# Moving the head-norm sums of an HGRN2 layer between two input-projection halves, in eight narrow matmuls instead of six wide ones

## The chip, the cores and the metric

The kernel runs on one core of a Trainium2 chip. The metric is the device time of one execution in microseconds; the kernel before was timed three times, with a median of 1609.88 us (1609.36 to 1610.61). Engines are called PE (matrix), DVE (vector), ACT (scalar), POOL and SP (the queue that starts most transfers).

## The reference, cut to what matters

One step of a two-layer encoder trunk for 256 + 64 = 320 frames, width 1024, in float32. Layer 0 is a mix of two recurrences and a dense feed-forward part; layer 1 is an HGRN2 recurrence and a top-2-of-8 expert feed-forward part. The change touches only the end of the HGRN2 mixer:

```
proj = h @ w_in_c                      # 1024 -> 4096: q, f, i, g, 8 heads of 128 each
o, s = chunk_gated_linear_attention(silu(q), k(f), i, log_f(f), s0)
o = o * rsqrt(mean(o*o over a head's 128) + 1e-5) * hgrn_norm_w      # rms_norm
out = (o * silu(g)) @ w_out_c          # 1024 -> 1024
```

## The kernel before, in words

Features lie on the 128 partitions, frames in the free dimension, so a head is one block of 128 x 320, and half of the heads (0 to 3 or 4 to 7) one block of 128 x 1280. Every dense matrix comes from memory in tiles of 1024 x 256. A tile is worked on in two halves (512 rows each): ACT rounds a half to a shorter float (`half_rounded`, line 1945), DVE subtracts it from the original (`half_rest`, line 1167), and PE takes three products, high by high, low input by high weight, high input by low weight (lines 518 to 520). A half is 24 matmuls of 320 columns. The input of a product is split in the same way: for the output projection ACT copies each head to its high part (`output_rounded`, line 2263) and DVE subtracts (`output_rest`, line 1658).

The input projection `in_c` has 16 tiles, 0 to 15, the output projection `out_c` four, which the code also counts on as 16 to 19. Tile 15 of `in_c` gives the last two heads of the gate g. The recurrence's steps are written between the halves of the tiles 8 to 15, the same order by hand on each engine. At its end DVE adds the parts of the output (`outputs_of(h)`, line 1642), ACT squares them (`squares(h)`, line 2248), PE sums the squares over the partitions by a matmul with a matrix of ones (`hgrn_sums(h)`, line 968), ACT takes Ln and then Exp with scale -0.5 (`root_mean(h)`, lines 2254 and 2258), DVE multiplies (`normed`, line 1648) and applies the gate (`gated`, line 1651). h is the half of the heads.

PE writes to eight banks of PSUM (a bank holds 512 columns of float32), and `take` hands them out in turn. It waits for a count on a semaphore that says that the bank's previous user has been read: the owner and the count are given when the bank is taken. `turn[0] += 2` skips two banks. The first two tiles of `out_c` take their four banks together, before the first of their matmuls. Semaphores are shared between stages; in the tables of order below `attention_b` counts the added outputs, `attention_osq` the squares, `attention_rms` what ACT has read or made of the sums, `in_c_done` the projected banks that ACT has emptied, `dense_lo` the weight halves ready, `in_lo` the heads split.

## Time and profile before

| | |
|---|---|
| median of three runs | 1609.88 us (1609.36 to 1610.61) |
| the profiled execution, its own time | 1610.61 us |
| its span from first to last instruction | 1608.8 us |
| PE busy | 1484.3 us (92% of the span) |
| DVE busy | 1161.5 us (72%) |
| ACT busy | 944.9 us (59%) |
| granted PE clock, mean over the span | 0.966 of full |
| HGRN2 end with `out_c` (716 to 762 us): PE busy | 42.97 of 46 us |

Times are from the start of the span. In rows of a timeline the columns are the start, the time from the first start to the last end of the merged instructions, the engine and line, the operation with output and inputs, the count, and in brackets how long the engine was idle before it and who released it. PE records of float32 matmuls with ones appear twice for each matmul of the program. "x12" at line 968 is six matmuls.

### The profile page before, as it was taken

The numbers are of one execution on the slowest core, as the hardware profiler recorded it, in microseconds if no ns is written. First come the engines' busy times: TensorE is split into PE (matmuls) and PEld (weight loads), VectorE is DVE, ScalarE is ACT, GpSimd is POOL, SyncE is SP. The second block draws the span as 40 slices with busy tenths as digits, with TensorE's granted clock in tenths as the row PEclk, the third lists the DMA queues.
The fourth block names the chain that finished last, engine by engine and source line by source line (L and its number), as shares of the span: only waits on it lengthen the run. The fifth ranks groups of instructions, "written<-read, shape, count | busy, mean of one in ns | idle before, by whom it ended". The sixth has DMA issues, their size and how long they took to land.

```text
span 1608.8 us, 28958 instructions
## 1 busy us (share of the span) xinstructions
PE 1484.3 (92%) x11188; PEld 1325.4 (82%) x11189; DVE 1161.5 (72%) x1562; ACT 944.9 (59%) x1238; POOL 75.2 (5%) x147
## 2 busy tenths in 40 slices
PE   7889967899999899999599999999999999999992
PEld 7879967799999798988477888887888888788881
DVE  5574846455543458965488898898889989898994
ACT  5453114433332468544467777877788777877872
POOL 8200000000000000000000000000000000000000
PEclk9999988999999999999689999999999999999996
DMA  8411002244444343322389999999999999999982
GB/s 245 149 53 57 4 2 76 87 142 156 157 138 151 106 131 119 106 80 89 132 328 352 398 367 390 381 357 396 332 398 366 382 387 344 396 335 404 367 299 80
DMA packets 162030, 371.70 MB, mean 231 GB/s; under 512 B 10152, under 2 KB 85840, under 8 KB 161936
## 3 DMA queue, kind: packets, MB, share of 16 engines
q1 hardware_dynamic: 159120, 360.14, 61.4%
q0 software_dynamic: 2448, 8.91, 2.1%
q8 instruction: 69, 1.13, 0.3%
q10 hardware_dynamic: 368, 1.31, 0.2%
q14 instruction: 25, 0.20, 0.0%
HBM read 360.10 MB, written 10.24 MB: 230 GB/s over the span
## 4 chain that ended last, share of the span: by engine, by line
PE 76%; DVE 12%; issue 6%; ACT 4%; DMA 1%; DVEq 0%; SPq 0%; POOLq 0%; POOL 0%; ACTq 0%
PE bank L1093 9%; PE bank L1094 9%; PE bank L1095 9%; PE bank L518 9%; PE bank L520 9%; PE bank L519 9%; DVE w_lo L1809 4%; PE bank L602 4%; PE bank L1117 3%; PE bank L1119 3%; PE bank L1118 3%; DVE wd_lo L1167 1%; PE bank L839 1%; PE bank L834 1%; PE bank L890 1%
## 5 line engine op out<-in xcount | busy, mean ns | idle before, releaser
L1809 DVE TENSOR_TENSOR w_lo<-moe_ring,w_hi 128x1024 fp32r<-128x1024 f32 (+1 forms) x560 | 608.0, 1156 | 42.4 <-ACT w_hi L2363 42.3
L2363 ACT ACTIVATE w_hi<-moe_ring 128x1024 fp32r<-128x1024 f32 (+1 forms) x560 | 532.6, 1014 | 84.3 <-PE bank L1119 51.6
L1167 DVE TENSOR_TENSOR wd_lo<-arena,wd_hi 128x1024 fp32r<-128x1024 f32 x142 | 171.0, 1208 | 189.2 <-ACT wd_hi L1945 188.8
L518 PE MATMUL bank<-in_hi,wd_hi 128*128 128x320 f32 x880 | 279.3, 317 | 23.6 <-DVE in_lo L1180 17.0
L1093 PE MATMUL bank<-w_hi,xe_hi 128*128 128x512 f32 (+1 forms) x768 | 288.6, 376 | 1.4 <-DVE xe_lo L1843 1.4
L1094 PE MATMUL bank<-w_hi,xe_lo 128*128 128x512 f32 (+1 forms) x768 | 286.6, 373 | 0.0
L1095 PE MATMUL bank<-w_lo,xe_hi 128*128 128x512 f32 (+1 forms) x768 | 286.1, 372 | 0.0
L519 PE MATMUL bank<-in_lo,wd_hi 128*128 128x320 f32 x880 | 275.6, 313 | 0.0
L520 PE MATMUL bank<-in_hi,wd_lo 128*128 128x320 f32 x880 | 275.4, 313 | 0.0
L1945 ACT ACTIVATE wd_hi<-arena 128x1024 fp32r<-128x1024 f32 x142 | 148.3, 1047 | 194.4 <-PE bank L520 185.9
L518 PEld LDWEIGHTS bank<-in_hi,wd_hi 128*128 128x128 f32 x880 | 168.8, 192 | 28.6 <-issue 21.7
L519 PEld LDWEIGHTS bank<-in_lo,wd_hi 128*128 128x128 f32 x880 | 169.0, 192 | 0.1
L520 PEld LDWEIGHTS bank<-in_hi,wd_lo 128*128 128x128 f32 x880 | 168.6, 192 | 0.0
L1093 PEld LDWEIGHTS bank<-w_hi,xe_hi 128*128 128x128 f32 x768 | 145.0, 189 | 27.5 <-DVE xe_lo L1843 1.8
L1095 PEld LDWEIGHTS bank<-w_lo,xe_hi 128*128 128x128 f32 x768 | 144.6, 188 | 26.1
L1094 PEld LDWEIGHTS bank<-w_hi,xe_lo 128*128 128x128 f32 x768 | 144.9, 189 | 25.1
L1117 PE MATMUL bank<-w_hi,gt_hi 128*128 128x512 f32 x256 | 101.2, 395 | 2.3 <-DVE w_lo L1809 2.3
L1119 PE MATMUL bank<-w_lo,gt_hi 128*128 128x512 f32 x256 | 99.8, 390 | 0.0
L1118 PE MATMUL bank<-w_hi,gt_lo 128*128 128x512 f32 x256 | 99.7, 389 | 0.0
L602 PE MATMUL bank<-arena 64*64 64x64 f32 (+1 forms) x2128 | 72.4, 230 | 16.3 <-DVE arena L1457 9.9
L602 PEld LDWEIGHTS bank<-arena 64*64 64x64 f32 x2128 | 70.3, 145 | 18.0 <-DVE arena L1457 10.3
L518 PE MATMUL bank<-hid_hi,wd_hi 128*128 128x320 f32 x240 | 74.2, 309 | 2.5 <-DVE hid_lo L1658 1.5
(354 smaller groups left out, 1721.4 us busy)
## 6 DMA issues: line engine op xcount, KB each, us to landing
moe_ring<-in_moe_w SPq DMA_DIRECT2D x216, 1024.0 KB, 8.4
moe_ring<-in_moe_w SPq DMA_DIRECT2D x64, 768.0 KB, 4.7
arena<-in_ffn_w SPq DMA_DIRECT2D x30, 1024.0 KB, 5.4
arena<-in_w_in_c SPq DMA_DIRECT2D x16, 1024.0 KB, 5.3
arena<-in_w_in_ab SPq DMA_DIRECT2D x13, 1024.0 KB, 5.9
arena<-in_w_out_ab SPq DMA_DIRECT2D x4, 1024.0 KB, 5.8
arena<-in_w_out_c SPq DMA_DIRECT2D x4, 1024.0 KB, 4.9
arena<-in_ffn_w SPq DMA_DIRECT2D x4, 768.0 KB, 4.2
```

Source lines behind the costliest of these rows:

```text
L518: pe.matmul(b[:, 0:T], w_[0][:, cols], x_hi, start=start, stop=False)
L519: pe.matmul(b[:, 0:T], w_[0][:, cols], x_lo, start=False, stop=False)
L520: return pe.matmul(b[:, 0:T], w_[1][:, cols], x_hi, start=False, stop=stop)
L602: mm = pe.matmul(b[rows, col:col + right.shape[-1]], left[rows], right[rows], start=start, stop=stop, skip_group_check=True)
L1093: pe.matmul(b[:, 0:w], xe_hi[:, k, :], hi_[:, c0:c1], start=(k == 0), stop=False)
L1094: pe.matmul(b[:, 0:w], xe_lo[:, k, :], hi_[:, c0:c1], start=False, stop=False)
L1095: mm = pe.matmul(b[:, 0:w], xe_hi[:, k, :], lo_[:, c0:c1], start=False, stop=(k == KC - 1))
L1117: pe.matmul(E_Y[half][:, :], g_hi[:, g], hi_[:, cols], start=first, stop=False)
L1167: dve.tensor_tensor(wd_lo[:, m_ % DENSE_UNITS, 0:words], src, wd_hi[:, m_ % DENSE_UNITS, 0:words], ALU.subtract).then_inc(S("dense_lo"), 1)
L1809: dve.tensor_tensor(w_lo[:, i % UNITS, 0:unit_words(i)], moe_unit(i), w_hi[:, i % UNITS, 0:unit_words(i)], ALU.subtract)\
L1945: act.activation(wd_hi[:, m_ % DENSE_UNITS, 0:words], src, ACT.Copy).then_inc(S("dense_hi"), 1)
L2363: act.activation(w_hi[:, i % UNITS, 0:unit_words(i)], moe_unit(i), ACT.Copy).then_inc(S("e_hi"), 1)
```

## The change

Both sums move and change shape. The six matmuls of 512, 512 and 256 columns for each half of the heads, which stood together between the halves of tile 15, become eight of 320 columns, one for each head: the first four stand before tile 15, the last four between its halves. The skip of two banks is gone. ACT's Ln follows with four instructions for each half instead of three. ACT rounds the first half of tile 16 between the two squares instead of after both; DVE forms its rest between the two `outputs_of`. ACT's `root_mean(1)` comes after `output_rounded(0, 4)` with a weight rounding inside, where before its three Ln came ahead of those copies. The last two gate heads are no longer copied out of PSUM by ACT and then run through Silu in place: Silu reads their two banks directly, later in ACT's order. DVE multiplies 128 x 1280 at once where it worked in pieces of 640.

```diff
-        READY_OUT = [1, 1, 2, 2, 3, 3, 4, 4]
-        RMS_PARTS = [(0, 512), (512, 1024), (1024, 4 * T)]
+        READY_OUT = [1, 1, 1, 1, 2, 2, 3, 3]
@@ PE
             def hgrn_sums(h):
                 pe.wait_ge(*at_count("hgrn_osq", h + 1))
-                squares_ = hz[:, heads_of(h)].rearrange("p f t -> p (f t)")
-                for i, (c0, c1) in enumerate(RMS_PARTS):
-                    b = take(("hgrn_rms", h, i), "hgrn_rms", 4 * h + i + 1)
-                    pe.matmul(b[:, 0:c1 - c0], ones[:, :], squares_[:, c0:c1], start=True, stop=True)\
-                      .then_inc(S("hgrn_rms_full"), 1)
+                for f in range(4 * h, 4 * h + 4):
+                    b = take(("hgrn_rms", f), "hgrn_rms", f + 1 + h)
+                    pe.matmul(b[:, 0:T], ones[:, :], hz[:, f, :], start=True, stop=True).then_inc(S("hgrn_rms_full"), 1)
                 else:
                     hgrn_inside(0)
                     hgrn_inside(1)
+                    hgrn_sums(0)
-            def both_sums():
-                hgrn_sums(0)
-                hgrn_sums(1)
-
-            in_c_parts(15, both_sums, lambda: None)
-            turn[0] += 2
+            in_c_parts(15, lambda: hgrn_sums(1), lambda: None)
             two = [[take(("out_c", 2 * i + j), "c_res", 2 * i + j + 1) for j in range(2)] for i in range(2)]
@@ DVE
             outputs_of(0)
+            rest_of(16, 0)
             outputs_of(1)
-            rest_of(16, 0)
+            normed(0)
             dve.wait_ge(*at_count("hgrn_silu", 3))
-            for f in (0, 2):
-                normed(f, f + 2)
-                gated(f, f + 2)
+            gated(0, 4)
             rest_of(16, 1)
             output_rest(0, 4)
-            normed(4, 6)
+            half_rest(2 * (OUTC_T + 1))
+            normed(1)
             gated(4, 6)
-            normed(6, HH)
-            half_rest(2 * (OUTC_T + 1))
-            dve.wait_ge(*at_count("hgrn_silu", 4))
+            dve.wait_ge(*at_count("in_c_done", 4 * KC))
             gated(6, HH)
             output_rest(4, KC)
@@ ACT
             squares(0)
+            half_of_in_c(16, 0)
             squares(1)
-            half_of_in_c(16, 0)
             root_mean(0)
             half_of_in_c(16, 1)
-            root_mean(1, lambda: output_rounded(0, 4))
-            in_c(15)
-            half_rounded(2 * (OUTC_T + 1))
-            silu_of(hg[:, 6:HH], 4 * KC)
+            output_rounded(0, 4)
+            root_mean(1, lambda: half_rounded(2 * (OUTC_T + 1)))
+            for j in (4 * KC - 2, 4 * KC - 1):
+                act.wait_ge(*at_count("in_c_full", j + 1))
+                act.activation(hg[:, j % KC, :], where["in_c", j][:, 0:T], ACT.Silu).then_inc(S("in_c_done"), 1)
             output_rounded(4, KC)
```

PE's order before, from the sums to the first matmul of the output projection (L968 the sums, L518 with `in_hi` the second half of tile 15, L518 with `hid_hi1` the first of `out_c`; brackets name the semaphores waited for):

```order
L968 MATMUL bank7<-arena,ones 128x512 [waits attention_b,attention_osq]
L968 MATMUL bank0<-arena,ones 128x512 [waits attention_b]
L968 MATMUL bank1<-arena,ones 128x256 [waits attention_b]
L968 MATMUL bank2<-arena,ones 128x512 [waits attention_b,attention_osq]
L968 MATMUL bank3<-arena,ones 128x512 [waits attention_b]
L968 MATMUL bank4<-arena,ones 128x256 [waits attention_b]
L518 MATMUL bank5<-in_hi,wd_hi 128x320 [waits dense_lo]
...
L518 MATMUL bank7<-hid_hi1,wd_hi 128x320 [waits attention_rms,dense_lo,in_lo]
```

The same stretch after the change, from the first sums on (L966 the sums, L517 the products):

```order
L966 MATMUL bank5<-arena,ones 128x320 [waits attention_b,attention_osq]
...
L966 MATMUL bank0<-arena,ones 128x320 [waits attention_b]
L517 MATMUL bank1<-in_hi,wd_hi 128x320 [waits dense_lo,attention_b]
...
L966 MATMUL bank3<-arena,ones 128x320 [waits attention_b,attention_osq]
L966 MATMUL bank4<-arena,ones 128x320 [waits attention_b]
L966 MATMUL bank5<-arena,ones 128x320 [waits attention_rms]
L966 MATMUL bank6<-arena,ones 128x320 [waits attention_rms]
L517 MATMUL bank1<-in_hi,wd_hi 128x320 [waits dense_lo]
...
L517 MATMUL bank7<-hid_hi1,wd_hi 128x320 [waits in_c_done,dense_lo,in_lo,attention_rms]
```

Tile 15 now sits in banks 1 and 2 and the four banks that `out_c` takes are 7, 0, 1 and 2; its first matmul has `in_c_done` among its waits, which it had not.

ACT's order before, from the Ln of the second half of the heads to the last output copies (L1945 rounds weights, L2043 copies tile 15 out, L2263 the output copies):

```order
L2254 ACTIVATE arena<-bank2,eps_norm 128x512 [waits attention_rms_full]
L2254 ACTIVATE arena<-bank3,eps_norm 128x512 [waits attention_rms_full]
L2254 ACTIVATE arena<-bank4,eps_norm 128x256 [waits attention_rms_full]
L2263 ACTIVATE hid_hi1<-arena 128x320 [waits attention_out] x4
L2258 ACTIVATE arena<-arena 128x1280 [waits attention_rms]
L2043 ACTIVATE arena<-bank5 128x320 [waits in_c_full]
L2043 ACTIVATE arena<-bank6 128x320 [waits in_c_full]
L1945 ACTIVATE wd_hi<-arena 128x1024 [waits in_c_full,tile_in0]
L2226 ACT_TABLE_LOAD
L2226 ACTIVATE arena<-arena 128x640 [waits in_c_done]
L2263 ACTIVATE hid_hi1<-arena 128x320 [waits attention_out] x4
```

The same stretch of ACT after the change (L2252 the output copies, L2243 Ln, L2247 Exp, L2329 Silu out of the two banks of tile 15):

```order
L2252 ACTIVATE hid_hi1<-arena 128x320 [waits attention_out] x4
L2243 ACTIVATE arena<-bank3,eps_norm 128x320 [waits attention_rms_full]
L2243 ACTIVATE arena<-bank4,eps_norm 128x320 [waits attention_rms_full]
L2243 ACTIVATE arena<-bank5,eps_norm 128x320 [waits attention_rms_full]
L2243 ACTIVATE arena<-bank6,eps_norm 128x320 [waits attention_rms_full]
L1935 ACTIVATE wd_hi<-arena 128x1024 [waits in_c_full,tile_in0]
L2247 ACTIVATE arena<-arena 128x1280 [waits attention_rms]
L2329 ACT_TABLE_LOAD
L2329 ACTIVATE arena<-bank1 128x320 [waits in_c_full]
L2329 ACTIVATE arena<-bank2 128x320 [waits in_c_full]
L2252 ACTIVATE hid_hi1<-arena 128x320 [waits attention_out] x4
```

The instructions that empty the banks of tile 15 stand behind the Exp and a table load, where the copies had stood ahead of both the rounding and the load; the first four output copies stand ahead of the four Ln instead of behind three.

## Rows read from the trace of the kernel before

**Rows 1.** Page, part 4: the chain that ended last, by engine.

```profile
PE 76%; DVE 12%; issue 6%; ACT 4%; DMA 1%; DVEq 0%; SPq 0%; POOLq 0%; POOL 0%; ACTq 0%
```

**Rows 2.** Timeline of PE, from the recurrence's end to the layer norm.

```profile
716.21 2.56 PE L957 MATMUL bank<-arena 64*64 64x64 f32 x160
719.29 0.39 PE L518 MATMUL bank<-in_hi,wd_hi 128*128 128x320 f32 x1 [0.51 <-DVE arena L1642]
...
722.89 4.46 PE L968 MATMUL bank<-arena,ones 128*128 128x512 f32 x12
...
730.55 0.31 PE L520 MATMUL bank<-in_hi,wd_lo 128*128 128x320 f32 x1
732.37 0.39 PE L518 MATMUL bank<-hid_hi,wd_hi 128*128 128x320 f32 x1 [1.51 <-DVE hid_lo L1658]
...
737.13 0.41 PE L518 MATMUL bank<-hid_hi,wd_hi 128*128 128x320 f32 x1 [1.01 <-DVE wd_lo L1167]
...
761.88 4.47 PE L834 MATMUL bank<-arena,ones 128*128 128x320 f32 x16
```

**Rows 3.** Timeline of ACT, the same stretch.

```profile
719.61 1.27 ACT L2248 ACTIVATE arena<-arena 128x1280 f32<-128x1280 f32 x1 [0.35 <-DVE arena L1642]
721.20 1.27 ACT L2248 ACTIVATE arena<-arena 128x1280 f32<-128x1280 f32 x1 [0.32 <-DVE arena L1642]
722.38 1.04 ACT L1945 ACTIVATE wd_hi<-arena 128x1024 fp32r<-128x1024 f32 x1
...
728.01 1.61 ACT L2254 ACTIVATE arena<-bank,eps_norm 128x512 f32<-128x512 f32 x3
729.50 0.84 ACT L2263 ACTIVATE hid_hi<-arena 128x320 fp32r<-128x320 f32 x2
...
734.33 1.28 ACT L2226 ACT_TABLE_LOAD   x1
735.62 0.74 ACT L2226 ACTIVATE arena<-arena 128x640 f32<-128x640 f32 x1
```

**Rows 4.** Timeline of DVE, the same stretch.

```profile
717.91 3.26 DVE L1642 TENSOR_TENSOR arena<-arena,bank 128x512 f32<-128x512 f32 x8
...
729.80 0.88 DVE L1651 SCALAR_TENSOR_TENSOR arena<-arena,vec 128x640 f32<-128x640 f32 x1
730.60 1.22 DVE L1167 TENSOR_TENSOR wd_lo<-arena,wd_hi 128x1024 fp32r<-128x1024 f32 x1
```

**Rows 5.** Groups by line and shape: busy us, mean ns of one.

```profile
L1588 DVE TENSOR_TENSOR arena<-arena 128x1280 f32<-128x1280 f32 x12 | 17.8, 1486 | 2.5 <-PE bank L890 2.5
L2094 ACT ACTIVATE arena<-bank,eps_norm 128x320 f32<-128x320 f32 x4 | 2.1, 514 | 0.9 <-PE bank L699 0.9
```

**Rows 6.** Line 2175, a Silu out of PSUM: min/median/max ns.

```profile
L2175 ACT ACTIVATE arena<-bank x22: 437/438/438, 318.2 to 460.1; 128x320 f32<-128x320 f32 x22
```

**Rows 7.** Waits of PE, 100 to 600 us: us in total, times, longest.

```profile
PE bank L518 <- DVE in_lo L1180: 17.0, 3, 6.1
...
PE bank L518 <- ACT lrow L2025: 3.5, 1, 3.5
```

**Rows 8.** Stretches: length, busy us (count) by engine, PEclk, DMA share, GB/s.

```profile
210.20:212.70 2.50, 0.00 (x0) 0.00 (x0) 2.47 (x7) 0.00 (x0) 0.00 (x0) 1.00 0.00 0
212.80:215.80 3.00, 3.00 (x56) 3.00 (x58) 1.16 (x2) 0.00 (x0) 0.00 (x0) 0.51 0.00 0
107.37:114.37 7.00, 7.00 (x38) 7.00 (x39) 6.93 (x8) 2.60 (x5) 0.00 (x0) 0.78 0.80 253
263.77:270.77 7.00, 7.00 (x36) 7.00 (x37) 4.20 (x9) 2.89 (x5) 0.00 (x0) 0.74 0.48 152
309.36:316.36 7.00, 7.00 (x30) 7.00 (x31) 4.16 (x8) 5.04 (x10) 0.00 (x0) 0.58 0.00 0
560.10:567.10 7.00, 7.00 (x34) 7.00 (x35) 4.27 (x9) 5.59 (x10) 0.00 (x0) 0.69 0.00 0
738.00:762.00 24.00, 24.00 (x165) 24.00 (x165) 10.66 (x16) 7.10 (x8) 0.00 (x0) 1.00 0.30 111
```

22 lines of the change are left out of this document (10 added, 12 removed).

## The prediction

> **What bounds the kernel now.** I read the page first. PE holds 76% of the chain that ended last, DVE 12% and ACT 4% [rows 1]: what counts is when PE may start its next product, and work on the two other engines counts only where PE waits for it. Then the timelines of the three engines around the change, which lies between 716 and 762 us. From 737.13 to 761.88 PE runs the rest of `out_c` without a gap: seven halves in 24.75 us, 3.54 us each [rows 2]. Everything after that hangs on it in a row (layer norm, router, experts), and no transfer starts in between that does not itself wait for these steps, so a microsecond at 761.88 is a microsecond at the end. Ahead of it PE has three gaps: 0.51 us before tile 15, 1.51 us before `out_c`, 1.01 us before its second tile [rows 2], 3.0 us in all. This is all that any new order here can win from waiting.
>
> **The change part by part.** All instructions up to the first Square, which starts at 719.61 [rows 3], are the same in both kernels, so I walk the new order on from there.
>
> *PE's own work.* The six sums start at 722.89 and take 4.1 us until the next product; the layer norm's x16 records, eight matmuls of 320 columns, take 4.47 us, 0.56 each [rows 2]. The eight new sums cost 4.5 us against 4.1, 0.4 us more, but the four before tile 15 and the rest stand ahead of a later wait, as will be seen, so this costs nothing.
>
> *Start of tile 15.* Before, PE was done with the recurrence at 718.8 and began tile 15 at 719.29 [rows 2]. Now it must first do sums for which the Square has to end: 719.61 + 1.27 = 720.88. Four sums, until 723.1. Tile 15 then needs banks 1 and 2, which DVE empties in the second `outputs_of`, and in DVE's queue the rest of tile 16 now stands ahead of that. The chain: the second Square began 1.18 after which the rounding followed (721.20 to 722.38), so the rounding starts at 719.61 + 1.18 = 720.79 and ends 1.04 later at 721.83 [rows 3]; DVE's rest takes 1.14 until the next instruction (730.60 and its 1.22 row [rows 4], less a small overlap) and ends its turn at 723.05; a `outputs_of` is half of 3.26 us [rows 4], and its two large pieces are about 1.27 of that: banks 1 and 2 are free at 724.3, all is added at 724.7. So tile 15 starts at 724.3 and not 719.29. First half until 727.9 (719.29 to 722.89 is 3.60), four sums until 730.1, second half until 733.7. PE is 2.8 us later than before (730.55 + 0.31 [rows 2]).
>
> *ACT's chain.* Second Square at 724.72, Ln from 725.90. Three Ln cover 1280 columns in 1.49 us (728.01 to 729.50), one instruction of 1280 columns takes 1.18 [rows 3]: each further instruction adds about 0.155, so four take 1.65. From the other side, four times the 514 ns of a lone one [rows 5] would be 2.06; I take 1.65, since they follow each other. The Exp waits for the last to end, 727.7, and ends at 728.95; the second rounding of tile 16 fits behind it. DVE multiplies 1280 columns in 1.49 [rows 5] and applies the gate; for this shape the trace has nothing, between 1.49 and twice 0.88 [rows 4]; I take 1.55: done at 732.2. ACT then copies four heads (two take 0.84 [rows 3], four about 1.5): 733.7. Four Ln: 735.35. Rounding of tile 17, whose wait for tile 15 (733.7) has 1.6 us to spare: 736.3. Exp, 1.26: 737.55. Table load, 1.28 [rows 3]: 738.84. Two Silu out of PSUM, 438 ns each [rows 6], overlapping by some 0.07: 739.65.
>
> *The bank wait, the heart of it.* Before, `out_c` took banks 7, 0, 1, 2, last used by sums that ACT had read before its copies at 729.50 [rows 3]. Tile 15 had banks 5 and 6. With the skip gone and two more sums, tile 15 is in 1 and 2, and `out_c` takes just these as its third and fourth before its first matmul. They are released by the two Silu, which are the last things in ACT's chain. So the first half of `out_c`, whose operands are there at about 734.1 (first head copied and subtracted), waits until 739.75. Queued behind it on PE are all eight halves of the four tiles, and for them wait the residual on DVE and the rounding of tiles 18 and 19 on ACT. What else must be there is not late: weights of tile 17, first half, 737.6 (needed 743.3); second half of the heads, subtracted by 742.4 (needed 746.8); last weight half, 743.9 (needed 750.4).
>
> *Sum without the clock.* 739.75 + 8 x 3.54 = 768.04 against 761.88: 6.16 us later. One of the eight halves ran before 737.13 in the old order, 3.54 us of the sum; the other 2.62 is the later restart.
>
> *The clock.* PE is idle from 733.7 to 739.75, 6 us. In this trace PE came to dense products after four such gaps, three that add up to 17.0 us (the longest 6.1) and one of 3.5 [rows 7], and each time the granted clock was at half (1.2 of 2.4 GHz) on restart: mean PEclk in the next 7 us 0.78, 0.74, 0.58 and 0.69, with 38, 36, 30 and 34 matmuls done [rows 8]. At the full clock 165 are done in 24 us, 48 in 7. Missing are 10, 12, 18 and 14, at 0.145 us 1.5, 1.7, 2.6 and 2.0 us. I expect the same here, mean 1.95. The Trainium skill ("TensorE: Matmul & The Clock Gate", the HAM clock gate) says that idleness throttles the array and that activity has to release it; the four restarts agree.
>
> Together 6.16 + 1.95 = 8.1 us. Against the profiled execution, 1610.61, this is 1618.7. That execution was the slowest of three, 0.73 above the median, so for the median I say 1609.88 + 8.1 = 1618.0.
>
> *Where a page speaks against a row.* The chain holds one table load. It takes 1.28 us here and the Silu follows at once, 734.33 to 735.62 [rows 3]. The Trainium skill ("ScalarE: Activation LUTs", What ACT_TABLE_LOAD costs) adds a drain of about 1.38 us to every switch. By the page the Silu would end at 741.0, and the total would be 1619.4; the row shows no such time, and the sum goes by the row.
>
> **The rivals.** I count within 0.2% (3.2 us) as no change that can be measured.
>
> *The bank wait does not decide (not slower).* If the two Silu did not hold the banks, the first half would start at 734.1, the second follow at 737.7 (weights of tile 17 are subtracted at 737.6), the third at 741.3, when the fifth head is subtracted, and the fourth end at 748.4, against 747.7 before (737.13 + 3 x 3.54): 0.7 us slower, 1610.6, no change. For it: only the order of one engine's queue makes the wait. Against it: ACT would have to be 5.6 us faster than its rows; it is a chain of nine instructions with known durations. The point from which it decides is 734.1.
>
> *Faster.* The first sums stand earlier, and the split at tile 15 could let PE fill its gaps. All three together are 3.0 us [rows 2], so at the very most 1606.9, just under 0.2%. It decides if `out_c` could start before 730.9; but the second Square is at 724.72 where it was at 721.20 [rows 3], and all that `out_c` needs is made behind it. I see no way.
>
> *The clock falls twice.* PE now also waits from 718.8 to 720.9 and from 723.1 to 724.3. After a stretch that short, 2.5 us without a matmul from 210.2 on, the clock was at half for the next three [rows 8]; against it, these two gaps are 2.1 and 1.2 us long. If the clock falls here, tile 15 runs at half for some us and ends up to 3 us later; 1.6 of this is covered by the slack before the rounding of tile 17, the rest, about 1.5, delays the Silu: 8.1 + 1.5, 1619.5.
>
> *The clock holds through the 6 us.* Then 6.2 us, 1616.0. Against it are four of four restarts.
>
> **How the numbers follow.** The forecast 0.57; the clock falls twice 0.24; the clock holds 0.08; the bank wait does not decide 0.06; the drain of the page 0.03; faster 0.02. Slower by over 0.2% are the forecast, both clock cases and the drain, 0.92; within 0.2% the wait that does not decide and half of the faster case, whose most is just under the bound, 0.07; faster 0.01. For the range: the clock's price is 1.5 to 2.6, my chain of nine steps may be off by 0.7 either way, runs differ by 1.25 us among themselves, and the double fall adds 1.5: low 6.16 + 1.5 - 0.7 - 1 = 6.0, high 6.16 + 2.6 + 1.5 + 0.6 = 10.9: 1615.9 to 1620.8; I open the low end to 1615.6 to hold the case in which the clock holds.
>
> **What would show it.** In the profile after: tile 15 begins near 724.3, behind the second `outputs_of` and not behind the sums; the first product of `out_c` begins near 739.8 and is released by ACT's Silu (line 2329), with about 6 us idle before it; after that PEclk is 0.5 for 3 to 6 us; the gap at the second tile of `out_c` is gone; the layer norm's sums begin near 770. I am wrong if PE's idle time ahead of `out_c` is released by DVE's `in_lo` or is under 3 us, or if the experts' part is shorter by what this part is longer.

## The result and the profile after

The kernel after takes 1621.07 us (median of five, 1619.69 to 1623.92), the kernel before 1610.61 us (median of five, 1609.36 to 1613.43): ratio 1.0066, 95% interval 1.0052 to 1.0082. It is slower, by 10.5 us where 8.1 were forecast, and the median lies 0.27 us above the high end of the range given. The profiled execution took 1620.02 us with a span of 1618.3 (before 1610.61 and 1608.8) and a mean clock of 0.963 (0.966).

The page of after, its busy time and the engines of the chain, against [rows 1] and the table of before:

```profile
PE 1490.6 (92%) x11192; PEld 1331.8 (82%) x11193; DVE 1161.7 (72%) x1559; ACT 944.4 (58%) x1239; POOL 74.8 (5%) x147
...
PE 75%; DVE 13%; issue 6%; ACT 4%; DMA 1%; DVEq 0%; SPq 0%; POOLq 0%; POOL 0%; ACTq 0%
```

These two lines hardly show that anything happened. DVE and ACT do the same work; PE's busy time grew by 6.3 us although it has two matmuls more, mostly because a matmul at half clock counts as busy for longer. The timeline of PE around the change, which answers to [rows 2], shows the loss:

```profile
715.93 2.57 PE L956 MATMUL bank<-arena 64*64 64x64 f32 x160
720.66 4.11 PE L966 MATMUL bank<-arena,ones 128*128 128x320 f32 x8 [2.15 <-ACT arena L2238]
...
728.13 2.31 PE L966 MATMUL bank<-arena,ones 128*128 128x320 f32 x8
730.04 0.55 PE L517 MATMUL bank<-in_hi,wd_hi 128*128 128x320 f32 x1
...
733.65 0.31 PE L519 MATMUL bank<-in_hi,wd_lo 128*128 128x320 f32 x1
739.65 0.61 PE L517 MATMUL bank<-hid_hi,wd_hi 128*128 128x320 f32 x1 [5.69 <-ACT arena L2329]
740.05 0.47 PE L518 MATMUL bank<-hid_lo,wd_hi 128*128 128x320 f32 x1
...
770.32 4.47 PE L833 MATMUL bank<-arena,ones 128*128 128x320 f32 x16
776.03 4.28 PE L838 MATMUL bank<-arena,ones 128*128 128x320 f32 x15 [1.25 <-ACT arena L2140]
```

The first product of `out_c` starts at 739.65 after 5.69 us of nothing, and the bracket names its releaser: line 2329, the Silu out of the two banks of tile 15. The same in the waits of PE from 714 to 775 us (total, times, longest), in which no other wait is over 2.2 us and before's 1.5 at `out_c` and 1.0 at its second tile are gone:

```profile
PE bank L517 <- ACT arena L2329: 5.7, 1, 5.7
PE bank L966 <- ACT arena L2238: 2.2, 1, 2.2
```

The timeline of ACT, answering to [rows 3], is the chain that ends in this release:

```profile
719.33 1.27 ACT L2238 ACTIVATE arena<-arena 128x1280 f32<-128x1280 f32 x1 [0.34 <-DVE arena L1635]
720.51 1.04 ACT L1935 ACTIVATE wd_hi<-arena 128x1024 fp32r<-128x1024 f32 x1
724.43 1.28 ACT L2238 ACTIVATE arena<-arena 128x1280 f32<-128x1280 f32 x1 [2.88 <-DVE arena L1635]
725.61 1.76 ACT L2243 ACTIVATE arena<-bank,eps_norm 128x320 f32<-128x320 f32 x4
727.40 1.27 ACT L2247 ACTIVATE arena<-arena 128x1280 f32<-128x1280 f32 x1
...
731.89 1.55 ACT L2252 ACTIVATE hid_hi<-arena 128x320 fp32r<-128x320 f32 x4 [2.27 <-DVE arena L1643]
733.35 1.75 ACT L2243 ACTIVATE arena<-bank,eps_norm 128x320 f32<-128x320 f32 x4
734.99 1.06 ACT L1935 ACTIVATE wd_hi<-arena 128x1024 fp32r<-128x1024 f32 x1
735.93 1.28 ACT L2247 ACTIVATE arena<-arena 128x1280 f32<-128x1280 f32 x1
737.23 1.28 ACT L2329 ACT_TABLE_LOAD   x1
738.52 0.77 ACT L2329 ACTIVATE arena<-bank 128x320 f32<-128x320 f32 x2
```

And the timeline of DVE, answering to [rows 4]; the rest of tile 16 now stands between the two `outputs_of`, and the gate of 1280 columns takes 1.55:

```profile
717.63 1.67 DVE L1635 TENSOR_TENSOR arena<-arena,bank 128x512 f32<-128x512 f32 x4
721.58 1.23 DVE L1160 TENSOR_TENSOR wd_lo<-arena,wd_hi 128x1024 fp32r<-128x1024 f32 x1 [2.28 <-ACT wd_hi L1935]
722.73 1.67 DVE L1635 TENSOR_TENSOR arena<-arena,bank 128x512 f32<-128x512 f32 x4
...
730.30 1.55 DVE L1643 SCALAR_TENSOR_TENSOR arena<-arena,vec 128x1280 f32<-128x1280 f32 x1
```

Stretches of after (length, busy time and count of PE, PE's weight loads, DVE, ACT and POOL, granted clock, DMA share, GB/s): the first sums, the first 7 us of `out_c`, the rest of it, and two stretches of the first expert's products, before and behind a wait of 2.3 us. [Rows 8] have the same for before.

```profile
720.66:724.66 4.00, 4.00 (x9) 2.58 (x10) 2.81 (x5) 1.12 (x2) 0.00 (x0) 0.57 0.39 124
739.65:746.65 7.00, 7.00 (x31) 7.00 (x32) 2.48 (x6) 2.34 (x5) 0.00 (x0) 0.61 0.00 1
746.65:770.00 23.35, 23.35 (x161) 23.35 (x160) 9.17 (x12) 5.76 (x6) 0.00 (x0) 1.00 0.28 106
817.96:867.60 49.64, 47.35 (x201) 38.74 (x201) 41.76 (x61) 38.12 (x41) 0.00 (x0) 0.94 0.97 376
867.60:912.05 44.45, 43.57 (x220) 36.78 (x220) 41.03 (x49) 32.13 (x40) 0.95 (x1) 0.96 0.95 354
```

The two stretches of the first expert in the kernel before, beside them:

```profile
809.64:858.51 48.87, 46.58 (x200) 38.16 (x201) 41.49 (x61) 38.07 (x41) 0.00 (x0) 0.96 0.98 378
858.51:901.65 43.14, 42.26 (x221) 35.56 (x221) 40.95 (x49) 32.13 (x40) 0.95 (x1) 1.00 0.96 357
```

So the two profiled executions differ like this. The code up to the first Square is the same, yet the Square starts at slightly other times from execution to execution (718.5 to 722.2 us over the profiles of this study that have no added matmuls ahead of it), so I measure from there. I call *the region* the time from the first Square to the second batch of the layer norm's sums: 719.61 to 767.59 before, 719.33 to 776.03 after, 47.98 and 56.70 us, **8.72 us longer**. Its end in the kernel before is this row:

```profile
767.59 4.55 PE L839 MATMUL bank<-arena,ones 128*128 128x320 f32 x16 [1.25 <-ACT arena L2150]
```

Of the 8.72 us, 2.39 is the clock: 739.65 to 770.32 is 30.67 us where eight halves at 3.54 take 28.28. The other 6.33 is the later start. Behind the region, layer norm and router take 41.93 instead of 42.05, the two stretches of the first expert 0.77 and 1.31 more, and the rest 0.9 less: 9.5 in span with the 0.28 by which the Square came earlier. The region is what the prediction was about; whether the 2.1 us in the first expert belong to the change is asked at the end of the experiments. (The 0.9 less at the end is within scatter: what follows the first expert's two stretches took 706.2 to 707.6 us over all profiles of this study.)

### The profile page after: what moved, and what is told of

Read it like the earlier page. It is cut to its first block, busy times and chain, and to the rows that moved or that the text cites. A ratio compares the mean times of both kernels' runs of the same rounds, so it can differ in the third digit from the quotient of the medians.

```text
span 1618.3 us, 28962 instructions
## 1 busy us (share of the span) xinstructions
PE 1490.6 (92%) x11192; PEld 1331.8 (82%) x11193; DVE 1161.7 (72%) x1559; ACT 944.4 (58%) x1239; POOL 74.8 (5%) x147
## 3 DMA queue, kind: packets, MB, share of 16 engines
q8 instruction: 69, 1.13, 0.3%
q10 hardware_dynamic: 368, 1.31, 0.2%
## 4 chain that ended last, share of the span: by engine, by line
PE 75%; DVE 13%; issue 6%; ACT 4%; DMA 1%; DVEq 0%; SPq 0%; POOLq 0%; POOL 0%; ACTq 0%
PE bank L1086 9%; PE bank L1087 9%; PE bank L1088 9%; PE bank L517 9%; PE bank L519 9%; PE bank L518 9%; DVE w_lo L1799 4%; PE bank L601 4%; PE bank L1110 3%; PE bank L1112 3%; PE bank L1111 3%; DVE wd_lo L1160 1%; PE bank L838 1%; PE bank L833 1%; PE bank L889 1%
## 5 line engine op out<-in xcount | busy, mean ns | idle before, releaser
L517 PE MATMUL bank<-in_hi,wd_hi 128*128 128x320 f32 x880 | 279.8, 318 | 23.1 <-DVE in_lo L1173 17.0
L518 PE MATMUL bank<-in_lo,wd_hi 128*128 128x320 f32 x880 | 275.8, 313 | 0.0
L517 PEld LDWEIGHTS bank<-in_hi,wd_hi 128*128 128x128 f32 x880 | 169.1, 192 | 28.2 <-issue 21.7
L518 PEld LDWEIGHTS bank<-in_lo,wd_hi 128*128 128x128 f32 x880 | 169.0, 192 | 0.3 <-issue 0.2
L517 PE MATMUL bank<-hid_hi,wd_hi 128*128 128x320 f32 x240 | 75.2, 313 | 5.7 <-ACT arena L2329 5.7
```

The source lines that it names most:

```text
L517: pe.matmul(b[:, 0:T], w_[0][:, cols], x_hi, start=start, stop=False)
L518: pe.matmul(b[:, 0:T], w_[0][:, cols], x_lo, start=False, stop=False)
```

## The experiments

Theory: `out_c` waits for banks that tile 15 used and that ACT's late Silu releases, and PE then runs at half clock. Rivals: the longer chain through ACT and DVE (each half of the heads squared, summed and gated in turn, with weight halves between) would delay `out_c` even with other banks; or the narrower sums, the wider gate, or something behind the region. Each median stands against runs of the kernel before on the same chip.

**e1: other banks for the second pair.** The kernel after, with the skip of two banks put between the two pairs that `out_c` takes.

```diff
-            two = [[take(("out_c", 2 * i + j), "c_res", 2 * i + j + 1) for j in range(2)] for i in range(2)]
+            two = []
+            for i in range(2):
+                two.append([take(("out_c", 2 * i + j), "c_res", 2 * i + j + 1) for j in range(2)])
+                if i == 0:
+                    turn[0] += 2
```

> The kernel after, with one thing undone: the second pair of banks that the output projection takes are 3 and 4 (two banks skipped between the pairs), so none of its four banks is one that tile 15 fills and the two Silu empty. Theory (the bank wait): the first product of the output projection starts near 734 us on the trace's clock of before instead of 739.8, PE's idle time there falls from 5.7 to under 1 us, the granted clock stays at full, the fourth half ends near 748.4 against 747.7 before: 0.7 us over before, 1611.3, that is 9 to 10 us below the kernel after. Rival (ACT's late chain holds the output projection by its operands, whatever bank it takes): the idle time stays at 5 us or more, released by DVE's in_lo, and the time stays at 1619 or more. Rival (the added and moved sums or the many small ACT instructions are the cost): stays within 2 us of the kernel after.

Measured: 1613.01 against 1610.91, ratio 1.0009 [1.0000, 1.0018]. The first product of `out_c` with the load of its weights (PEld), from the timeline:

```profile
734.93 0.19 PEld L517 LDWEIGHTS bank<-hid_hi,wd_hi 128*128 128x128 f32 x1 [0.91 <-ACT arena L2247]
734.96 0.38 PE L517 MATMUL bank<-hid_hi,wd_hi 128*128 128x320 f32 x1 [0.68 <-DVE hid_lo L1654]
```

The wait is down from 5.69 to 0.68 us. The two rows name different releasers. The split of the first head (`hid_lo`) had been done since 733.7; what ended last is ACT's second Ln of the second half (line 2247), which reads bank 4 until 734.60, and banks 3 and 4 are the pair that this kernel takes. So what is left is again a wait for a bank, a short one. The region is 49.24, so of the 8.72 only 1.26 is left. This one choice of banks was worth 7.5 us in the region and some 8 in the median. The rival that the chain alone does it is out, except for at most that 1.26. The median is 2.1 us above before where I had expected 0.7; the twelve executions fall into two groups, to which the section on the prediction comes back.

**e2: the skip taken out of the kernel before.**

```diff
             in_c_parts(15, both_sums, lambda: None)
-            turn[0] += 2
             two = [[take(("out_c", 2 * i + j), "c_res", 2 * i + j + 1) for j in range(2)] for i in range(2)]
```

> The kernel before without its skip of two banks, all else the same: the output projection takes banks 5, 6, 7 and 0, where 5 and 6 are those of tile 15, emptied by ACT's two copies at 732.6 to 733.4 us. Theory (a bank wait costs only what it holds beyond the other waits): the first half starts near 733.4 instead of 732.4, the second still at 737.1, since it waits for weights: 0 to 0.3 us over before. Rival (sharing the banks of tile 15 is what costs, whoever empties them and when): 3 us or more over before.

Measured: 1612.12 against 1610.91, ratio 1.0007 [0.9999, 1.0016]; region 47.97, as before. The wait at `out_c` grew from 1.5 to 2.6:

```profile
734.26 0.19 PEld L518 LDWEIGHTS bank<-hid_hi,wd_hi 128*128 128x128 f32 x1 [2.83 <-ACT arena L2042]
734.29 0.39 PE L518 MATMUL bank<-hid_hi,wd_hi 128*128 128x320 f32 x1 [2.60 <-DVE hid_lo L1657]
```

The product's row names the split, but its first head was split by 733.07; the weight load names the last to end, ACT's two copies out of the banks of tile 15 (line 2042, 733.45 to 734.19). So here too `out_c` waits for tile 15's banks, 1.1 us longer than in before. The first half starts later, but the second then follows without before's gap of 1.01 [rows 2]. The wait for these banks costs nothing as long as it is no longer than the next wait behind it; the banks are dangerous only together with a late release.

**e3: the wait stays, PE kept busy in it.** The kernel after, with nine matmuls of ones by a constant into the first of the banks before its use; they may start once ACT has read that bank's sum, the third of the eight, which is long before, so they follow tile 15 at once.

```diff
+            def keep_warm(b, n):
+                for _ in range(n):
+                    pe.matmul(b[:, 0:T], ones[:, :], reset[:, :], start=True, stop=True)
...
             in_c_parts(15, lambda: hgrn_sums(1), lambda: None)
+            pe.wait_ge(*at_count("hgrn_rms", 3))
+            keep_warm(bank[turn[0] % 8], 9)
```

> The kernel after with nine more float32 matmuls of 320 columns of constants, 5 us of PE work in the 5.7 us wait ahead of the output projection, into its first bank, overwritten afterwards. Theory (the wait costs twice, once as a wait and once as a low clock behind it): the start at 739.7 stays, the granted clock is 1.00 in the 7 us behind it where it was 0.61, and the output projection ends 2.4 us earlier: 1618.5 or so, 2 to 3 us below the kernel after. Rival (the low clock in that stretch is not due to the idle time, or the layer norm behind takes the gain away): no change against the kernel after.

Measured: 1617.83 against 1610.91, ratio 1.0045 [1.0032, 1.0058]. Its timeline of PE at the wait:

```profile
732.93 5.00 PE L524 MATMUL bank<-reset,ones 128*128 128x320 f32 x18
738.82 0.38 PE L517 MATMUL bank<-hid_hi,wd_hi 128*128 128x320 f32 x1 [0.88 <-ACT arena L2336]
```

and its first 7 us of `out_c`, in the columns of the stretches above:

```profile
738.82:745.82 7.00, 7.00 (x48) 7.00 (x49) 3.71 (x7) 3.97 (x6) 0.00 (x0) 1.00 0.00 1
```

The release by the Silu (here line 2336) is the same, the clock is full, 48 matmuls instead of 31 are done in 7 us, and the region is 54.27: 2.43 shorter than in after. The clock's term, seen by taking it away, is 2.4 us. The wait's term, which is left, is 6.3. The medians say the same more roughly: 6.9 us above before where after is 10.5 and 10.0 (e7) above it. (The profiled execution, 1613.44, is the fastest of the five by 3.6 us; the region is taken from it alone, and it is 2 us short in the router as well, see the last section.)

**e4: the old order of the weight half, with the new banks.** The kernel after, with tile 16's first half rounded behind both squares and its rest formed behind both `outputs_of`.

```diff
             outputs_of(0)
-            rest_of(16, 0)
             outputs_of(1)
+            rest_of(16, 0)
@@ ACT
             squares(0)
-            half_of_in_c(16, 0)
             squares(1)
+            half_of_in_c(16, 0)
```

> The kernel after with the rounding of tile 16's first half behind both squares on ACT, and its rest behind both outputs_of on DVE, as before; the bank wait stays. Theory (the Silu that release the banks end a chain through ACT and DVE, and putting this piece of work between its links lengthens it by the round trip): the second Square starts at 721.2 instead of 724.4, the Silu end near 737, PE restarts at 737.0 instead of 739.7, still with an idle time of over 4 us and a low clock behind it: 2.5 to 3 us below the kernel after, about 1618. Rival (the chain is set by the sums on PE, which still wait for tile 15): PE restarts within 1 us of 739.7 and the time stays.

Measured: 1617.21 against 1610.91, ratio 1.0043 [1.0030, 1.0056]; region 54.64, 2.06 less than after. The second Square is 3.45 us earlier, yet the Silu only 0.9, and the first product comes at 738.76. I had expected 737.0 for it, so this expectation was wrong by 1.8 us. Of the 2.06, 0.95 is the earlier start; the other 1.11 is the clock, since behind this shorter wait of 4.75 us 39 matmuls are done in 7 us, not 31. Its timeline of ACT shows where the chain now stands still:

```profile
720.98 1.27 ACT L2238 ACTIVATE arena<-arena 128x1280 f32<-128x1280 f32 x1 [0.32 <-DVE arena L1635]
...
728.45 1.06 ACT L1935 ACTIVATE wd_hi<-arena 128x1024 fp32r<-128x1024 f32 x1 [1.75 <-PE bank L519]
729.91 1.55 ACT L2252 ACTIVATE hid_hi<-arena 128x320 fp32r<-128x320 f32 x4 [0.41 <-DVE arena L1643]
...
734.11 1.06 ACT L1935 ACTIVATE wd_hi<-arena 128x1024 fp32r<-128x1024 f32 x1 [0.98 <-PE bank L519]
...
737.64 0.77 ACT L2329 ACTIVATE arena<-bank 128x320 f32<-128x320 f32 x2
```

ACT's chain now waits twice for tile 15 on PE (brackets 1.75 and 0.98, 2.7 us together), since a weight half may only be rounded once its buffer has been used up. Tile 15 is late here because the four sums ahead of it ran at a low clock, as in after; there ACT was as late itself and it did not matter. What the low clock costs in this order is read from e5 and e8 below: 1.6 us, most of the 1.8 that this expectation missed.

**e5: both, other banks and the old order.** The edits of e1 and e4 together.

```diff
+                if i == 0:
+                    turn[0] += 2
...
             outputs_of(1)
+            rest_of(16, 0)
...
             squares(1)
+            half_of_in_c(16, 0)
```

> Both undone together: other banks for the second pair, and the first rounding of tile 16 and its rest behind both squares and both additions, as before; the eight narrow sums in two places, the late copies and the Silu out of PSUM stay. Theory (those two hold all of the loss in waiting): the second tile of the output projection follows the first without a gap, the fourth half ends near 746.7 against 747.7 before: 1.0 us under before, 1609.9 against 1610.9. Rival (eight sums and four more small ACT instructions cost by themselves): 2 us or more over before.

Measured: 1610.24 against 1609.93, ratio 1.0001 [0.9992, 1.0010]; region 48.34, 0.36 above before, where I had expected about 1.0 below; no wait over 0.3 us is left at `out_c`. What this kernel still has of the change (eight narrow sums for six wide ones, the sums ahead of tile 15, the gate in one piece, Silu straight out of PSUM, four Ln) costs nothing that can be measured in the time, and brings nothing either.

The profile of e8 below, which has the same code in this stretch, shows what was missing. The first four sums in e5 and, second, in e8:

```profile
721.30 4.11 PE L966 MATMUL bank<-arena,ones 128*128 128x320 f32 x8 [2.17 <-ACT arena L2242]
```

```profile
717.09 2.42 PE L972 MATMUL bank<-arena,ones 128*128 128x320 f32 x8 [1.75 <-ACT arena L2250]
```

In e5 the clock fell in the wait ahead of them (0.56 from 721.30 to 725.20) and tile 15 began 4.90 us after the first Square; in e8 it held (1.00) and tile 15 began 3.33 us after it. The Silu follow 18.26 us behind the first Square in e5 (18.25 in e4) and 16.64 in e8. The region of e8 is 46.70, 1.64 shorter than in e5 and 1.28 shorter than in before. So the new form of the sums is the shorter one when the clock holds ahead of them. This is one profile; the medians below don't show such a gain.

**e12: the second pair taken late.** The kernel after, with its banks and order, but the pair in banks 1 and 2 waited for only behind the first half of the first tile.

```diff
-            two = [[take(("out_c", 2 * i + j), "c_res", 2 * i + j + 1) for j in range(2)] for i in range(2)]
+            two = []
             for h in range(2):
                 for i in range(2):
+                    if h == 0:
+                        two.append([take(("out_c", 2 * i + j), "c_res", 2 * i + j + 1) for j in range(2)])
                     dense_half(two[i], OUTC_T + i, h, 4, 2 * i, "out_c_full")
```

> The kernel after, but the second pair of banks (1 and 2, emptied by the Silu) is taken only behind the first half of the output projection's first tile. Theory (what the wait costs is what PE has queued behind it): the first half runs from 734 to 737.6 in the old wait, the second starts at 739.7, PE's idle time is about 2 us and the clock may hold: 2.6 us over before without the clock, up to 5 with it, that is 6 to 8 us below the kernel after. Rival (the first half can't start earlier than the Silu for another reason, its operands): as the kernel after.

Measured: 1614.41 against 1610.16, ratio 1.0031 [1.0020, 1.0042], 4.3 us above before; the wait for the same Silu (here line 2331) and the first product in its PE views:

```profile
PE bank L517 <- ACT arena L2331: 1.9, 1, 1.9
```

```profile
735.61 0.31 PE L517 MATMUL bank<-hid_hi,wd_hi 128*128 128x320 f32 x1
```

The first product follows tile 15 at once. The banks are released as late as in after, but 3.54 us of work no longer stand behind the release, and behind the 1.9 us that remain the clock is at 1.00. The region is 50.50, 2.52 above before, and 6.2 below after: with the same late release, the price of such a wait depends on what is queued behind it. (The median lies 1.7 us further above before than the region does, as in after; the profiled execution, 1611.37, is the fastest of the seven.)

**e7: the kernel after again, unchanged, on another chip.**

> The kernel after once more, to settle the 1.8 us between its median (10.5 over before) and what its stretch from the first Square to the layer norm explains (8.7). If the rest is scatter of the clock's phase in the first expert, where the wait of 2.3 us for a weight half was followed by a low clock in two of six profiles: this median lies between 8.7 and 10 over before, and a new profile may show that wait with the clock held. If it is a part of the change outside that stretch: again 10.5 or more, with the same low clock there.

Measured: 1619.97 against 1609.93, ratio 1.0057 [1.0044, 1.0070]. Wait 5.74 us, region 56.87; the first expert's stretches 49.84 and 44.46. The same picture, half a microsecond less in the median.

**What the clock's price is elsewhere.** If a long wait costs about 2 us through the clock alone, it costs that in the kernel before too.

**e6: PE kept busy in three waits of before.** Nine, eight and eight such matmuls ahead of the first tiles of `out_ab`, `h1` and `in_c` [rows 7].

```diff
-            def dense_pair(i, stage, name, j0, full, taken):
+            def dense_pair(i, stage, name, j0, full, taken, warm=0):
                 two = [take((name, j0 + j), taken, j0 + j + 1) for j in range(2)]
+                keep_warm(two[0], warm)
...
-                dense_pair(OUT_T + i, 1, "out_ab", 2 * i, "out_ab_full", "ab_res")
+                dense_pair(OUT_T + i, 1, "out_ab", 2 * i, "out_ab_full", "ab_res", 0 if i else 9)
```

> The kernel before with extra float32 matmuls of constants (320 columns, 0.56 us each) in the waits of 6.1, 5.4 and 5.4 us ahead of three dense stages, 9, 8 and 8 of them, into a bank that the stage then overwrites. Theory (a long wait ahead of dense products costs a second time by the clock): the granted clock stays 1.00 behind these three, 1.7 + 2.6 + 2.0 = 6.3 us less: near 1604.6. Rival (the clock falls whatever PE does there, or the extra matmuls delay the stage): no change or slower.

Measured: 1604.37 against 1609.93, ratio 0.9962 [0.9949, 0.9975]. The three stretches in e6, all at the full clock:

```profile
255.00:269.00 14.00, 11.80 (x57) 9.44 (x58) 10.07 (x16) 10.96 (x21) 0.00 (x0) 1.00 0.38 114
298.00:317.00 19.00, 17.46 (x91) 14.66 (x92) 12.18 (x25) 16.32 (x32) 0.00 (x0) 1.00 0.02 3
549.00:568.00 19.00, 17.87 (x103) 15.74 (x102) 10.87 (x19) 12.84 (x25) 0.00 (x0) 1.00 0.18 54
```

In before they have a clock of 0.76, 0.82 and 0.82. 5.6 us for three places is 1.9 each, the size that the prediction took from [rows 8]. Here the fillers sit in front of products whose start another engine decides, so they delay nothing.

**e9: PE kept busy in three waits of the router.**

```diff
             layer_norm("c")
+            keep_warm(bank[(turn[0] - 2) % 8], 9)
...
+            pe.wait_ge(*at_count("xtok_done", 6))
+            keep_warm(bank[(turn[0] - 4) % 8], 8)
             pe.wait_ge(*at_count("chosen", 1))
...
             chosen_rows(1)
+            keep_warm(bank[0], 10)
```

> The kernel before with extra float32 matmuls of constants in three waits around the router alone: 9 behind the layer norm, 8 ahead of the ranking, 10 in the gather of the first expert's rows; nothing added ahead of the dense stages. Theory (the low clock from the layer norm to the first expert costs some microseconds of transposes, logits and first products): 3 to 5 us below before. Rival (e8 gained there only because its dense part had moved the clock's phase): within 1 us of before.

Measured: 1605.95 against 1610.16, ratio 0.9977 [0.9968, 0.9986]; 4.2 us below before, 1.4 for each of the three waits. In the profile, layer norm and router take 38.77 us instead of 42.05, at a clock of 0.87 instead of 0.64; the first expert's first stretch takes another 1.8 less (47.04) and its second 1.3 more (44.46):

```profile
766.85:805.62 38.77, 35.17 (x174) 27.72 (x174) 19.51 (x59) 16.72 (x31) 1.28 (x1) 0.87 0.30 111
```

**e8: e5 with the fillers of e6 and e9.**

```diff
                 two = [take((name, j0 + j), taken, j0 + j + 1) for j in range(2)]
+                keep_warm(two[0], warm)
...
             layer_norm("c")
+            keep_warm(bank[(turn[0] - 2) % 8], 9)
```

> The kernel with order and banks undone (e5) plus the extra matmuls ahead of the three dense stages (as e6) and in three waits around the router: 9 behind the layer norm, 8 ahead of the ranking, 10 in the gather of the first expert's rows. Theory (clock): 1.0 from e5, 6.3 from the dense stages, and in the stretch from the layer norm to the first expert, where half of the matmuls run at half the clock, 3 to 6 us: 1598 to 1601. Rival (that stretch is bound by ACT, DVE and a gather, not by PE's clock): 1603 to 1604.

Measured: 1600.56 against 1609.93, ratio 0.9939 [0.9926, 0.9952]; the gains add up, on the new form of the sums as on the old.

**The rest of the 10.5 us.** The region explains 8.7. First theory: what follows reacts to the later start by more than the delay itself.

**e10 and e11: a pure delay in the kernel before.** 15 (e10) or 8 (e11) filler matmuls between `out_c` and the layer norm, 8.4 and 4.5 us of PE at the full clock.

```diff
+            pe.wait_ge(*at_count("c_res", 1))
+            keep_warm(bank[turn[0] % 8], 15)
             layer_norm("c")
```

> The kernel before with PE kept busy for 8.4 us (15 extra float32 matmuls of 320 columns) between the output projection and the layer norm: a pure delay of all that follows, about as long as the change's, with nothing else moved. Theory (the 2 us that the change costs beyond its own stretch come from where the clock's fall meets the first expert, and a delay of that length does the same): 8.5 us in place and 2 us more, 10 to 10.5 over before, and in the profile the first expert lasts 44.4 and not 43.1 us behind its wait of 2.3 us. Rival (a delay is passed on as it is, the 2 us are from somewhere else): 8.4 to 8.7 over before.

> The same with 8 extra matmuls, 4.5 us. Theory (where the clock's fall meets the first expert is a matter of the moment, and a delay of another length may miss it): 4.5 us over before, as the two kernels with 6.3 and 6.7 us of delay did. Rival (any delay brings the 2 us): 6.5 over before.

Measured: e10 1618.55 and e11 1614.36 against 1610.16, ratios 1.0055 [1.0041, 1.0068] and 1.0031 [1.0018, 1.0043]: 8.4 and 4.2 us, with regions 8.09 and 4.31 us longer than in before. A delay here comes out at the end as it is, and the stretch behind the 2.3-us wait was 43.14 as in before. The theory fell.

**e13 and e14: no fall of the clock in the first expert.** In the profiles of after, e7, e1, e8 and e9 the clock fell at the 2.3-us wait in the first expert (44.42 to 44.46 us for the stretch behind it), in before, e2 to e6 and e10 to e12 it did not (43.11 to 43.14). Three fillers before the wait, in after (e13) and before (e14):

```diff
                     if s == 1:
+                        if not later:
+                            keep_warm(E_Y[0], 3)
                         down(0, range(KC))
```

> The kernel after with three extra float32 matmuls of 320 columns (1.7 us) in the wait of 2.3 us of the first expert, behind which both profiles of the kernel after show a low clock that costs 1.3 us. Theory (that low clock is a part of what the change costs): the clock stays at 1.00 there, the stretch behind the wait lasts 43.1 us instead of 44.4, and the kernel is 1.3 us below the kernel after: 8.7 to 9.2 over before. Rival (the rest above 8.7 is scatter between executions): 10 or more over before, or as much gained by the same edit on the kernel before.

> The same three matmuls in the kernel before, whose profile shows the clock at full behind that wait. Theory (the fall there comes with the change only): no change, within 0.5 us of before. Rival (the kernel before has the fall in part of its executions too): up to 1.3 us below before.

Measured: e14 1611.03 against 1611.31, ratio 0.9997 [0.9988, 1.0006]; e13 1620.75, ratio 1.0053 [1.0040, 1.0067]. In e13 the clock held, the stretch behind the wait is back at before's length:

```profile
868.60:911.75 43.15, 42.22 (x221) 35.56 (x221) 40.96 (x49) 32.14 (x40) 0.95 (x1) 1.00 0.94 354
```

and yet the whole is 9.4 us above before, not clearly below the 10.5 and 10.0 of the other two comparisons. So this fall is at most a part of the rest. Another part is in the stretch ahead of that wait, which the fillers leave alone: 49.63 us in e13, as in after (49.64), against 48.87 in before. Its first 8 us show why, first in after and then in before:

```profile
817.96:825.96 8.00, 8.00 (x24) 6.38 (x25) 6.67 (x10) 4.94 (x5) 0.00 (x0) 0.65 0.75 247
```

```profile
809.64:817.64 8.00, 8.00 (x27) 6.46 (x28) 6.83 (x11) 5.36 (x6) 0.00 (x0) 0.75 0.75 247
```

PE begins this stretch at the low clock in both, and in after it rises later: the mean over these 8 us is 0.65 against 0.75, with 24 matmuls against 27. In e1, e7 and e13 it is 0.61, 0.63 and 0.65. The region of e13 is 56.70, so region and this stretch make 8.72 + 0.76 = 9.5 us, and 9.4 were measured.

**e15: all fillers in the kernel before.** The lines of e6, e9 and e14 together.

```diff
+                keep_warm(two[0], warm)
...
+            keep_warm(bank[(turn[0] - 2) % 8], 9)
...
+            keep_warm(bank[(turn[0] - 4) % 8], 8)
...
+                            keep_warm(E_Y[0], 3)
...
+            keep_warm(bank[0], 10)
```

> The kernel before in its own order with all of the extra matmuls: three dense stages, three waits around the router, the wait in the first expert. If the gains add up: 5.6 (dense) + 4.2 (router) + up to 1.3: 1599 to 1600 where before is 1610; if the one in the first expert only matters with the others (both profiles with a busy router show its low clock): 1 us below e8's 9.4.

Measured: 1601.18 against 1611.31, ratio 0.9932 [0.9918, 0.9945]; the mean clock of its executions is 0.978 to 0.982, where before's on that chip have 0.966 to 0.971. With e8, whose interval overlaps with it, this is the best version run, 10.1 us under before and some 20 under after: as much as the whole change cost, gained by work whose result nobody reads.

## Why the prediction was wrong in size, by its own steps

*PE bound by its waits, ACT's chain decides: right.* The first product of `out_c` was forecast at 739.75 released by the Silu and came at 739.65, released by it, with 5.69 us of idle time (6.05 forecast). The steps on the way: tile 15 at 724.17 (724.3), its end at 733.96 (733.7; its first half 3.96 for 3.6, the last four sums 1.91 for 2.2), second Square 724.43 (724.72), gate done 731.85 (732.2), copies 733.4 (733.7), four Ln at 735.1 (735.35; 1.76 and not 1.65), Exp ended 737.21 (737.55), load 738.51 (738.84), Silu 739.29 (739.65). The chain was 0.3 us quicker than worked out, mostly because the first Square came 0.28 earlier, and the release reached PE 0.36 after the Silu's end, for which the prediction had 0.10: the two small errors cancel. e1 shows that the banks are the cause, e12 that what is queued behind the wait is the price, and e4 that the round trip between the engines is a further cause, worth 2.1 us where the banks of tile 15 are waited for. With other banks it is worth 0.9 (e1 against e5), nearly all of it the short wait for bank 4.

*The wait, 6.16: right.* Without the clock's share the layer norm's sums would have begun at 767.93, 6.05 us after before's 761.88; counted from the Square, which came 0.28 earlier, it is 6.33.

*The clock, 1.95: too small.* It cost 2.39 by the rows and 2.43 by e3. The four restarts of [rows 8] gave 1.5 to 2.6, and I took their mean. The profile of after shows 31 matmuls in its first 7 us and no transfer (DMA share 0.00). The two restarts of [rows 8] without a transfer have 30 and 34; their mean gives 2.3 us, and those two would have been the better rows, though no run here tests whether the transfers are the reason. This is the term of the sum that was mis-sized, by 0.44 us.

*Rivals.* That the bank wait doesn't decide, that it is faster, that the clock holds: out. The clock did fall twice: in the stretch from 720.66 it was 0.57, between the two levels of 1.2 and 2.4 GHz and near the lower. But it cost next to nothing at the end. Four sums took until 724.17 instead of 723.1, and banks 1 and 2, worked out for 724.3, were free only about then, as the load of tile 15's first weights shows, which waited for DVE's additions and not for the sums:

```profile
724.10 0.34 PEld L517 LDWEIGHTS bank<-in_hi,wd_hi 128*128 128x128 f32 x1 [0.20 <-DVE arena L1635]
```

From the second product of tile 15 on the clock was full. I had priced this at 1.5 us with tile 15 at half clock. Where DVE and ACT are not as late, the same fall does cost 1.6 us (e5 against e8). The Trainium skill ("ScalarE: Activation LUTs", What ACT_TABLE_LOAD costs) adds a drain of 1.38 us to a table switch. The load took 1.28 and the Silu began 0.01 us behind it; this case does not bear the drain out, and the row was right.

*A microsecond at 761.88 is one at the end, and nothing else is added there: this is the step that failed.* For a pure delay it is right: e10 and e11 show 8.4 us at the end for 8.09 in the region and 4.2 for 4.31. But the prediction put at nothing what the kernel does behind the region. The median is 3.1 us above the forecast of 1618.0. Of this 1.74 lies behind the region (10.46 against 8.72), 0.73 is the base, and 0.61 is the region itself (8.72 against 8.11: the clock 0.44, the wait 0.17). In the profile of after the part behind the region is the first expert: 0.77 us in its first stretch, where the clock rises later, and 1.31 behind the wait of 2.3 us, where it falls again; in e7 they are 0.97 and 1.32. With the fillers of e13 the second is gone, the first stays, and the whole is 9.4.

The clocks of the single executions point the same way. Of the twelve of e1, six with a mean clock of 0.963 or 0.964 took 1613.5 to 1615.1 us, and the profile, taken of one of them, has both extra pieces (49.91 and 44.44 us); six with 0.966 to 0.968 took 1609.9 to 1612.6. All six of after had 0.963 or 0.964. In e7 three had 0.963 and took 1620.0 to 1623.3, and two with 0.965 and 0.966 took 1618.6 and 1618.3, which is 8.7 and 8.4 above before, about what the region alone gives. None of the 73 executions of the kernel before that were run beside the experiments was under 0.966. That the extra is in most executions of after and in about half of those of e1 is therefore likely, but the two pieces themselves were seen only in the profiles. Noise alone isn't quite excluded either: 8.72 us is a ratio of 1.0054, inside the intervals of all three comparisons, though all three medians (10.5, 10.0 and, for e13, 9.4) lie above it. Why the change brings the first expert's clock into this state stays open; a pure delay does not (e10).

*The base and the range.* I took the profiled execution for a slow one and went down by 0.73 to the median of three, and the median of five was 1610.61 again. The high end of the range allowed 0.6 us for everything besides the wait, the clock's price and the double fall, while single executions of one kernel lie 4 us apart (1609.36 to 1613.43). With the base alone set right, the result would have been inside the range, and the step above would have been wrong all the same.

## What to carry to other kernels

When work that empties a PSUM bank moves later in an engine's queue, look up who takes that bank next and how many matmuls are queued behind its wait: here two Silu held the four tiles of the output projection, 28 us of work, and taking the second pair one half later (e12) or from other banks (e1) gave back 6 to 8 us. A long wait of PE (here 4.8 to 6 us) costs twice, once itself and once 1.3 to 2.4 us in the clock, so try filler matmuls in it before anything else: in six such waits (e6, e9) they gave together 0.6% of this kernel. And an edit that only frees one of two equally late engines gives back less than its own chain says (e4: the second Square came 3.4 us earlier, the Silu 0.9). When a profile row names a releaser that had ended long before, look at the row of the weight load and at what else had to be free (e1, e2).

## What the runs showed of the hardware

- Filler matmuls of 320 columns in a wait held the granted clock at 1.00 in each of the three dense places (e6) and at `out_c` (e3), even with 0.88 us (e3) and 1.13 to 1.25 us (e6) of idle time left behind the last of them. The Trainium skill ("TensorE: Matmul & The Clock Gate", the HAM clock gate) says that activity releases the clock; the runs agree, and show that activity whose result is unused does as well.
- Whether the clock falls at a wait of about 2.3 us is not fixed: the same stretch behind the same wait took 44.4 to 44.5 us in five of the fourteen profiles without fillers there (after, e1, e7, e8, e9) and 43.1 in the other nine. Behind the waits of 1.75 us in e8 and 1.9 in e12 it was 1.00; behind the one of 2.15 that ends at 720.66 in after it was 0.57.
- Single executions of one kernel scatter by 4 to 6 us (before 1609.36 to 1613.43, e3 1613.44 to 1619.43), and identical code before the change ends up to 3.7 us apart. One place of the scatter is the layer norm and router: 39.9 and 39.8 us at a clock of 0.70 in the profiles of e3 and e12, 41.8 to 42.1 in the others without fillers there, 0.64 in before. Differences under 2 us between two profiles have to be measured from a common point, as the region was here.
